# Regrouping the score tiles of the differential heads and moving projection units between them, in a two-layer decoder trunk on one TensorE

## What is computed

```
u = rms_norm(h, norm_pre[layer]);  proj = u @ w_in[layer]
y_a = mla_branch(...)     * silu(a_g)   # latent attention
y_b = dilated_branch(...) * silu(b_g)   # three dilated windows
y_c = sparse_branch(...)  * silu(c_g)   # top-128 keys by an indexer's score
y_d = diff_branch(...)    * silu(d_g)   # softmax map 0 minus lambda * softmax map 1
y = concat([y_a, y_b, y_c, y_d]) @ w_out[layer]
h = h + rms_norm(y, norm_post[layer])
```

## Time and profile before

| | |
|---|---|
| median of three runs | 719.69 us (718.64 to 719.76) |
| the profiled execution: its own time | 717.92 us |
| its span | 716.1 us |
| TensorE matmuls, busy | 676.5 us, 94% of the span, 3840 instructions |
| VectorE busy | 432.3 us, 60% |
| ScalarE busy | 330.3 us, 46% |
| GpSimd busy | 242.1 us, 34% |

### The profile page before, as it was taken

The page is one execution under the profiler, slowest core; times in us unless marked ns, Lnnn a source line. Parts: engine busy times, 40 slices in busy tenths (PEclk is TensorE's granted clock), DMA queues, the critical chain, the costliest instruction groups (busy, mean ns, idle before and its releaser), DMA issues. The chain is left out here.

```text
span 716.1 us, 10494 instructions
## 1 busy us (share of the span) xinstructions
PE 676.5 (94%) x3840; PEld 545.0 (76%) x3840; DVE 432.3 (60%) x1068; ACT 330.3 (46%) x751; POOL 242.1 (34%) x209
## 2 busy tenths in 40 slices
PE   6999999999999998799999999999999999978996
PEld 4888887887897754369998897788889776445896
DVE  4313897899797554640470269888978865456114
ACT  5424535653434637742353264465533354666121
POOL 1432633335055612002424536125323663200030
PEclk9999999999999969999999999999999997899999
DMA  8458876332322101112363598442322221030202
GB/s 249 131 176 244 231 215 237 95 107 67 111 85 85 59 1 58 60 27 95 118 177 110 178 257 230 123 132 74 105 75 74 79 70 59 0 118 1 90 28 91
DMA packets 66644, 80.96 MB, mean 113 GB/s; under 512 B 10737, under 2 KB 52337, under 8 KB 66593
## 3 DMA queue, kind: packets, MB, share of 16 engines
q1 hardware_dynamic: 66593, 80.29, 36.6%
HBM read 69.76 MB, written 13.93 MB: 117 GB/s over the span
## 5 line engine op out<-in xcount | busy, mean ns | idle before, releaser
L652 POOL TENSOR_TENSOR w_low<-w_raw,w_high 128x512 fp32r<-128x512 f32 (+2 forms) x156 | 199.2, 1309 | 383.2 <-ACT w_high L692 383.2
L1184 PE MATMUL bank<-uT,w_high 128*128 128x512 f32 x400 | 160.0, 400 | 0.2 <-DVE staging L998 0.2
L1186 PE MATMUL bank<-uT,w_low 128*128 128x512 f32 x400 | 158.3, 396 | 0.0
L1185 PE MATMUL bank<-uT,w_high 128*128 128x512 f32 x400 | 158.1, 395 | 0.0
L800 ACT ACTIVATE probs<-probs,negmax 128x128 f32<-128x128 f32 (+3 forms) x160 | 89.1, 559 | 95.7 <-DVE negmax L1039 95.4
L1184 PEld LDWEIGHTS bank<-uT,w_high 128*128 128x128 f32 x400 | 75.5, 189 | 18.6 <-issue 1.3
L1186 PEld LDWEIGHTS bank<-uT,w_low 128*128 128x128 f32 x400 | 75.4, 189 | 17.8
L1185 PEld LDWEIGHTS bank<-uT,w_high 128*128 128x128 f32 x400 | 75.5, 189 | 16.2
L692 ACT ACTIVATE w_high<-w_raw 128x2048 fp32r<-128x2048 f32 (+2 forms) x39 | 72.7, 1865 | 26.1 <-DMA w_raw<-in_w_out 23.1
L1184 PE MATMUL bank<-w_high,mix 128*128 128x256 f32 x256 | 72.4, 283 | 1.0 <-DVE mix L1124 1.0
L1186 PE MATMUL bank<-w_high,mix 128*128 128x256 f32 x256 | 71.6, 280 | 0.0
(11 more groups left out here) (150 smaller groups left out, 1089.4 us busy)
## 6 DMA issues: line engine op xcount, KB each, us to landing
w_raw<-in_w_in SPq DMA_DIRECT2D x27, 1024.0 KB, 5.4
w_raw<-in_w_out SPq DMA_DIRECT2D x8, 1024.0 KB, 4.9
parts_dram<-staging SPq DMA_DIRECT2D x12, 512.0 KB, 4.9
strips<-strips_dram SPq DMA_DIRECT2D x24, 256.0 KB, 4.4
dqk<-parts_dram SPq DMA_DIRECT2D x24, 256.0 KB, 4.4
hX<-in_x SPq DMA_DIRECT2D x8, 512.0 KB, 6.0
qidx<-parts_dram SPq DMA_DIRECT2D x12, 256.0 KB, 4.2
w_raw<-in_w_in SPq DMA_DIRECT2D x4, 512.0 KB, 5.4
```

What stands on the lines that cost most here:

```text
L652: ins = nc.gpsimd.tensor_tensor(w_low[:, s, ks, 0:w], w_raw[:, s, ks, 0:w], w_high[:, s, ks, 0:w].bitcast(F32), ALU.subtract)
L1184: nc.tensor.matmul(out_ap, lh, rh, start=start, stop=False)
L1185: nc.tensor.matmul(out_ap, lh, rl, start=False, stop=False)
L1186: return nc.tensor.matmul(out_ap, ll, rh, start=False, stop=stop)
```

## The change

D's tiles go in groups of 3, 3 and 2 instead of 2, 3, 2 and 1, in slots 0 to 3. From the second gate unit of B (`gb 1`) on, each unit stands one place earlier: before, slot 1 had `gb 1` and `ckv`, slot 2 both `bq`, slot 3 both `bk`, slot 4 `cqq 0`, slot 5 `cqq 1` and both `ck`; after, slot 0 ends with `gb 1`, slot 1 has `ckv` and `bq 0`, slot 2 `bq 1` and `bk 0`, slot 3 `bk 1` and `cqq 0`, slot 4 `cqq 1`, slot 5 both `ck`. `bq 0` is cut in two: a new step `part bq 0` makes the first 12 of its 24 matmuls ahead of the last two tiles of job 1, and `unit bq 0` the other 12 behind them. The selection rounds are placed anew; at the start of slot 6 the number done is the same as before, 37. From slot 6 on the order is the same. The places where ScalarE and GpSimd convert weights follow from the order: `bq`'s at `gb 1`, `bk`'s at `bq 0`, `cqq`'s at `bq 1` and `ck`'s at `bk 1`, as before; `bv`'s moves from `pv 2` to `cqq 1`, earlier in slot 4.

```diff
-    scores 0 0 2, topk 2, unit gd 1, scores 0 2 5, unit gb 0, scores 0 5 7, topk 1, scores 0 7 8
-    scores 1 0 2, norm 0, unit gb 1, topk 1, scores 1 2 5, turn 0 0, turn 0 1, topk 1, unit ckv 0, topk 1, scores 1 5 7, topk 1, turn 0 2, turn 0 3, scores 1 7 8, topk 1
-    scores 2 0 2, norm 1, unit bq 0, scores 2 2 5, turn 1 0, turn 1 1, topk 2, unit bq 1, scores 2 5 7, pv 0, topk 1, turn 1 2, turn 1 3, scores 2 7 8
-    scores 3 0 2, norm 2, topk 3, unit bk 0, turn 2 0, turn 2 1, scores 3 2 5, topk 2, unit bk 1, scores 3 5 7, pv 1, turn 2 2, turn 2 3, scores 3 7 8, dsquares 0
-    scores 4 0 2, norm 3, dscale 0, topk 1, unit cqq 0, turn 3 0, turn 3 1, scores 4 2 4, dnorm 0, pv 2, topk 2, turn 3 2, turn 3 3, topk 2, norm 4
-    scores 5 0 2, topk 1, unit cqq 1, topk 1, unit ck 0, topk 1, turn 4 0, turn 4 1, scores 5 2 4, topk 3, unit ck 1, topk 1, pv 3, turn 4 2, turn 4 3, dsquares 1, topk 2
+    scores 0 0 3, topk 3, unit gd 1, scores 0 3 6, topk 2, unit gb 0, scores 0 6 8, topk 2, unit gb 1
+    scores 1 0 3, norm 0, topk 1, unit ckv 0, scores 1 3 6, topk 1, turn 0 0, turn 0 1, part bq 0, scores 1 6 8, topk 1, unit bq 0, turn 0 2, turn 0 3
+    scores 2 0 3, norm 1, topk 1, unit bq 1, scores 2 3 6, topk 2, turn 1 0, turn 1 1, unit bk 0, scores 2 6 8, topk 1, pv 0, turn 1 2, turn 1 3
+    scores 3 0 3, norm 2, topk 1, unit bk 1, scores 3 3 6, topk 2, turn 2 0, turn 2 1, unit cqq 0, scores 3 6 8, pv 1, topk 1, turn 2 2, turn 2 3, dsquares 0
+    scores 4 0 2, norm 3, dscale 0, topk 2, unit cqq 1, turn 3 0, turn 3 1, scores 4 2 4, dnorm 0, pv 2, topk 3, turn 3 2, turn 3 3, norm 4
+    scores 5 0 2, topk 2, unit ck 0, turn 4 0, turn 4 1, scores 5 2 4, topk 2, unit ck 1, pv 3, topk 1, turn 4 2, turn 4 3, dsquares 1, topk 2
...
-                if (l, step) == (0, ("scores", 0, 0, 2)):
+                if (l, step) == (0, ("scores", 0, 0, 3)):
                     spread_rows(0, STRIP_ROW["D"])
...
+                if kind == "part":
+                    name, c = step[1:]
+                    g = l * NG + GI[name]
+                    s = g % SLOTS
+                    pe.wait_ge(w_low_done, g + 1)
+                    b = work_bank(l * NU + UNIT_AT[("unit", name, c)])
+                    cs = slice(c * P, (c + 1) * P)
+                    for k in range(4):
+                        three(b, w_high[:, s, k, cs], w_low[:, s, k, cs], uT[:, 0, k, :], uT[:, 1, k, :], k == 0, False)
...
-                    for k in range(4 if name == "cv" else 0, KC):
+                    for k in range(4 if name == "cv" or ("part", name, c) in UNIT_AT else 0, KC):
```

## The result

The changed kernel takes 723.35 us (median of 20 runs, 718.92 to 730.58), the kernel before 718.35 us (median of 20 runs beside it, 713.80 to 722.35). The ratio is 1.007, with a 95% interval from 1.0044 to 1.0096: slower by 5.0 us, under one per cent but clear of the noise. The one slow launch, 730.58, is left out of the ratio. The forecast was 724.0, which was 4.3 us more than the 719.69 of the kernel before that it started from. The profiled execution of the changed kernel took 720.34 us, with a span of 718.5.

The account below looks back on a forecast made before the run. TensorE, with matmuls under way 94% of the span, was taken as the bound. New waits 11.4 less old 10.0 and 0.3 gave +1.1 us, plus 3.2 for clock falls: +4.3, 724.0 us, range 716.2 to 728.0.

Parts of the forecast that it names:

- The old wait goes: Slot 0: TensorE's single 1.22 us wait for line 1039 vanishes, because a unit now stands between tile 7 and the next job.
- the waits of layer 0: Layer 0, first D score to slot 6: old waits the change could win, put at 4.1 us.
- the smaller waits: Waits beside the 1.22 us one, within 2.4 us counted in the first stretch and 1.7 us per layer in the second.
- The weights of `bq` in layer 0: Load lands just before 120.0, no earlier than before; `part bq 0` waits 2.0 to 3.0 us, taken as 2.5.
- my walk: The prediction's step-by-step timing of the new order, slots 0 to 5, from instruction durations and waits between engines.
- Norms against GpSimd: Norms 0 and 1 beside GpSimd conversions: a fully blocked norm costs 6.0 us against 2.45, nearly one wait per pass.
- The rival in which norms slip between the subtractions: Norms 0 and 1 pay only 1 us extra each; -3.5, 716.2 us, faster; chance 0.25.
- Norms 2 to 4 stay free: No conversion beside norm 2, norm 3 early by 0.2 us, norm 4 by 1.1; the second stretch's 1.7 us per layer go.
- VectorE as the bound: Rival: blocked norm 1 puts VectorE 3.5 us back, norms 2 to 4 wait 1 us each; +10, 730; chance 0.09.
- first stretches longer and second ones about as long: Sign of being right: first D score to `bq 0` start lengthens; from there to slot 6 stays about equal.
- the old fall of layer 1: Kernel before, layer 1's first stretch: clock fall behind the 1.22 us wait, about 1.6 us, counted among the old 10.0.
- The clock's term: Four new idle times of 2.1 to 3.0 us; two clock falls of 1.6 us each behind them, 3.2 us.

## Why the prediction was right

The mechanism was right; that the size came so near is in part luck, as the sum below shows.

**The old wait goes.** Right: no wait for line 1039 in slot 0 in any trace of the changed kernel. What the new order is worth without its new waits can be seen in the version with both norms early and strips late, which gains 3.1 us in layer 0 with no clock fall on either side. That is less than the 4.1 us at which the prediction put the waits of layer 0, though only 0.6 us of idle time are left in it; the smaller waits that the prediction counted in were too many. What the 1.22 us wait is worth by itself, no run shows.

**The weights of `bq` in layer 0.** Right in kind: they did not come earlier. The load kept its place and the data were there at 120.7 (forecast 120.0); GpSimd ran from 122.70 for 5.74 us, 0.7 more than undisturbed, because two passes of the norm met it. Norm 0's wait was forecast at 1.0 and the weights' at 2.5; measured were 1.67 and 1.37. The sum, 3.0 against 3.5, is what counts: VectorE came to norm 0 at 121.56 and not at 120.8, the four passes with two of them blocked took 4.0 us where my walk had some 3.1, and the later the turns, the less is left to wait for the weights.

**Norms against GpSimd.** This was the term on which the sign hung, and it held: 6.0 us forecast for a fully blocked norm, and 6.5 measured for norm 1 in layer 0, both with the reciprocal ahead of it. It divides otherwise: the four passes took 5.0 us where 5.3 were put, and what stands ahead of them 1.5 where 0.7 were put, because the small operation of line 940 was blocked too, for 1.0 us. The wait at the turns was forecast at 2.1 and measured at 2.21 in both layers; norm 0 of layer 1 at 3.0, measured 2.47. The Trainium skill's rule (page "SBUF — State Buffer", section "SBUF: two separate sides": an exclusive lock between GpSimd operations and VectorE operations with two SBUF inputs) agrees with each line of the interleaved timeline. The rival in which norms slip between the subtractions at 1 us extra each is refuted by the same lines. The lines add how the two take turns here: GpSimd's next pass goes ahead of VectorE's next, so that short passes pay again and again.

**Norms 2 to 4 stay free.** Right: 1.94 us for norms 2 and 3 in both layers, and none of the waits of the earlier trace rows for them is left. VectorE as the bound did not come about; its gap ahead of `bk 0`'s emptying absorbed the 4.0 us (6.2 against 2.2) that a blocked norm 1 takes more, and in layer 0 2.0 us of that gap were left.

**The stretches, cut at the start of `bq 0`.** One sign that was named did not come: first stretches longer and second ones about as long. In the first trace `part bq 0` began at 128.50 and 476.12, which makes 29.30 and 28.44 us before it (28.69 and 30.50 in the earlier trace rows) and 69.37 and 69.96 behind it (67.59 and 67.60). The cut is not like for like, because four tiles and two turns that stood ahead of `bq 0` now stand behind its start, and the blocked norm 1 lies behind the cut as well. Only the stretches up to slot 6 as a whole can be compared.

**The sum.** Forecast were +1.1 us from waits, with the old fall of layer 1 counted among the old losses, and +3.2 from two falls in the changed kernel. The first trace has one fall, in layer 1, so by the prediction's terms it should be 1.1 + 1.6 = 2.7 us longer; measured are 2.39 in layer 0 and 0.30 in layer 1, together 2.7. The layers share it otherwise than forecast: layer 0 was to be 1.7 longer (5.95 less 4.1 less 0.15), layer 1 1.0 (5.45 less 5.9 less 0.15, plus the fall). The two errors, 0.7 too little and 0.7 too much, cancel, and that is luck. In layer 0 the part up to the turns of job 0, without norm 0's wait, took 25.3 us where my walk had 24.7 (VectorE reached its first tile 5.6 us behind the first D score and not 5.3); and of the old small waits that were to go, less went than was counted. In layer 1 norm 0 waited 2.47 for 3.0, and the fall cost 1.3 for 1.6: turns of job 0 to turns of job 1 took 17.24 us, against 15.95 in layer 0 of the run with the strips late, which has no fall.

The clock's term was a mean over launches: one, three and four falls in three traces, 2.7 on average, where two were taken. With 2.7 falls the prediction's own sum is 1.1 + 4.3 = 5.4, against 5.5 between the traces' means and 5.0 between the medians. Taken apart, with each fall at its measured cost, I estimate the falls at 4.1 us a launch in the changed kernel and 1.6 before, so that 3.0 of the 5.5 us are waits (forecast 1.1 + 1.6 = 2.7) and 2.5 are falls (forecast 3.2 - 1.6 = 1.6). So the term that was most out of size is the number of falls, by 0.7 of one.

What is not shown is why a given wait is followed by a fall and the next is not; the traces show falls behind 8 of 12 of the new waits (counting norm 0 and the weights of layer 0 as one) and behind 2 of 4 of the 1.22 us waits before. With the variants counted in, it is 15 of 24 waits of about 2 us and more against 4 of 7 waits of 1.2 to 1.4 us. So these traces do not show that the longer wait makes the fall likelier; what the new order certainly does is to make more such waits.

## What to carry to other kernels

When work moves between engines' queues, ask of each elementwise operation which GpSimd operations run beside it, not only whether its inputs are there. The operations here that were blocked pass by pass have two SBUF operands, but the plain norm of the earlier trace rows, which reads one tensor of probabilities, took 4.62 us for 1.27 as well. The block is paid per instruction: many short passes beside a stream of GpSimd passes cost about one GpSimd pass each (1.2 to 1.6 us here). A wait of one or two microseconds on TensorE is paid a second time when the clock falls behind it (1.3 to 1.6 us here, and twice that where it stayed low for 7 us), so a reordering is judged on several traces. And where two causes stand one behind the other, as the blocked norm and the late weights in layer 0, remove both in one run before calling either harmless.

## What the runs showed of the hardware that I had not expected

A VectorE operation on 4 elements a row took 1.22 to 1.34 us when it came at the start of a GpSimd pass, and 0.42 to 1.13 when less of the pass was left, against 0.22: it pays for the rest of the pass that it meets, however small it is itself.

The granted clock behind slot 6 moves the launch time by more than this change does. From slot 6 to the first matmul of the output projection the order is the same in all kernels, yet it took 116.0 to 116.4 us in most traces, 117.5 to 119.2 in some, and 120.6 to 121.2 in both layers of two of them (norm 1 early and groups only), where the clock was at 1.2 GHz for longer (granted 0.90 on average, against 0.94 in the changed kernel's first trace). That is why the kernel with only norm 1 moved took 725.83 us in its one launch, though its two stretches are together 3.4 us shorter than those of the changed kernel's first trace. The two layers of a launch mostly share the longer or shorter form. Not every fall there stands behind a listed wait, and no run shows what sets them off.
